# Pooling layer of a three-layer transformer: the trailing mean as one product of 144 columns per token block, on top of a zero product

## The chip, the cores and the metric

The kernel runs on one core of a Trainium2 chip. The metric is the device time of one execution in microseconds; the shown time is the median of three runs. One further execution was profiled, and all rows below are from it.

## The reference, cut to what matters

Three layers run one after the other on 512 tokens of 1024 channels. The change touches the mixer of the third one, the pooling layer: per group of 256 channels a trailing mean over 2, 4, 8 or 16 tokens, minus the token itself, then a 256x256 map and a scale per channel.

```python
def mixer_pool(h, w_groups, scale):
    c = jnp.cumsum(hf, axis=1)
    count = jnp.arange(1, S + 1, dtype=jnp.float32)
    for gi, w in enumerate(POOL_WINDOWS):              # 2, 4, 8, 16
        sl = slice(gi * POOL_GROUP, (gi + 1) * POOL_GROUP)
        cg = c[..., sl]
        lag = jnp.pad(cg, ((0, 0), (w, 0), (0, 0)))[:, :S]
        mean = (cg - lag) / jnp.minimum(count, float(w))[None, :, None]
        outs.append(mean - hf[..., sl])
    pooled = jnp.stack(outs, axis=2).astype(h.dtype)
    y = jnp.einsum('bsgc,gcd->bsgd', pooled, w_groups).reshape(B, S, D)
    return y * scale
...
    h = h + rmsnorm(m, g[1])
    u = rmsnorm(h, g[2])
    h = h + rmsnorm(swiglu(u, ...), g[3])
```

## The kernel before, in words

The kernel is one long program for five engines, written out by hand: `FLOW` lists the stages, each engine has its own queue of instructions for every stage, and semaphores tie the queues together. Activations lie channels first: 8 tiles (`m`) of 128 channels by 512 tokens. Weights come in 233 units of 128x1024 numbers. SyncE loads a unit into one of four buffers `raw`. ScalarE makes its high part (`split_hi`, L818) and counts `hi_done`. VectorE makes the low part by subtraction (`split_lo`, L1330) and counts `lo_done`, which TensorE waits for and which frees the `raw` buffer for the unit four further on. In one earlier stage GpSimd makes some of the low parts (L757). A weight product of this kind has operands of type float32r (the number type whose products TensorE makes in one pass); operands of plain float32 take two passes, so each such product in the source is two matmul rows in the trace.

The pooling layer (`pool_layer` in the queues of ScalarE, VectorE and TensorE) does the map first and the mean afterwards. `linear(half, g)` maps two token blocks of 128 for a group, with tokens as output rows. `z_out(half, g)` moves the mapped block out of PSUM to `zt`, times the row's reciprocal root mean square: L994 on ScalarE, L1605 on VectorE, shared out by the table `ACT_Z`. Each z_out counts `zc_act` or `zc_dve`. Then, for each of the eight channel tiles `m`, TensorE multiplies `zt` with `band`, a banded matrix of plain float32 that holds the mean and the subtracted token: the main product covers the 128 columns of a block's own tokens (L2535), and the carry product covers the first 16 columns of the next block, which the block's last tokens reach into (L2539). The first product of a tile clears the PSUM bank. This part is called the averaging loop below. Before the first product of tile `m`, TensorE waits for `zc_act` and `zc_dve` up to group `m // 2` of the second half.

Behind each tile, ScalarE squares it (L852), and VectorE adds the square to a sum (L1339) and copies the first four tiles out (L1941). When the sum is complete, TensorE adds it over the channels (L2153), ScalarE takes the root (L1021, L1023), VectorE scales and adds the residual (L1616, L1620), ScalarE prepares the operand of the next stage (L1031), and TensorE starts on that stage (L2139). Between, TensorE runs products whose results nobody reads (`keep_clock`, L2119).

The units of the stage behind the pooling layer are counted from `FIRST["pool"] + 2`. They are called unit +2, +3, +4 and so on here. +2 to +4 are what `keep_clock` and the first products of the next stage read. They are split inside the pooling layer.

Of the kernel before, what the change touches and what calls it, by code (L numbers as in the profile page):

```python
# [27 lines left out]
P = 128  # L28
S = 512
# [9 lines left out]
NB = S // P  # L39
# [4 lines left out]
NPOOL, MAXW = 4, 16  # L44
GW = D // NPOOL
RAW, SPL = 4, 2
# [4 lines left out]
FIRST, COUNT, ORDER = {}, {}, [p[0] for p in PHASES]  # L51
# [70 lines left out]
def build(nc, xT, vecs, conv, sinks, w_alpha2, pe, cmp_w1, cmp_w2, weights, yT, flow=FLOW):  # L122
    f32, f32r = mybir.dt.float32, mybir.dt.float32r
    ALU, ACT, AX = mybir.AluOpType, mybir.ActivationFunctionType, mybir.AxisListType
# [4 lines left out]
    with ctx:  # L129
        def sb(name, shape, dt=f32, where=ctx):  # L130
            return where.enter_context(nc.sbuf_tensor(name, shape, dt))
# [5 lines left out]
        raw = [sb(f"raw{i}", [P, WU * P]) for i in range(RAW)]  # L137
# [11 lines left out]
        convw = sb("convw", [P, 4 * 2 * KF])  # L149
        epsc = sb("epsc", [P, 32])  # L150
        invc = sb("invc", [P, MAXW])

        ffn = ExitStack()
        ahi = sb("ahi", [P, KF * S], f32r, ffn)
# [8 lines left out]
        band = sb("band", [P, 2 * NPOOL, P + MAXW], f32, ffn)  # L163
# [211 lines left out]
        def whigh(n):  # L375
            if n == 2:
                return oh[:, 0:WU * P]
            if n == POOL_1:
                return map_pieces(alo, 8)
            if n in KEPT:  # L380
                return hhi[:, KEPT[n] * WU * P:KEPT[n] * WU * P + WU * P]
            return ahi[:, (16 + 2 * EXTRA[n]) * S:(18 + 2 * EXTRA[n]) * S] if n in EXTRA else whi[n % SPL][:, :]

        def wlow(n):
            if n == 2:
                return ol[:, 0:WU * P]
            if n == POOL_1:
                return map_pieces(alo, 12)
            if n in KEPT:
                return hlo[:, KEPT[n] * WU * P:KEPT[n] * WU * P + WU * P]  # L390
            return alo[:, (16 + 2 * EXTRA[n]) * S:(18 + 2 * EXTRA[n]) * S] if n in EXTRA else wlo[n % SPL][:, :]
# [265 lines left out]
        def _(pool):  # L657
# [5 lines left out]
            def fill(ins):  # L663
                n_filled[0] += 1
                ins.then_inc(filled, 1)

                pool.wait_ge(filled, n_filled[0])
# [4 lines left out]

            fill(pool.memset(ones[:, :], 1.0 / D))
            fill(pool.memset(epsc[:, :], EPS))
            fill(pool.memset(ident[:, :], 0.0))
            select(ident[:, :], [[-1, P]], 0, 1, ALU.not_equal, 1.0).then_inc(const_0, 1)
            for c in range(MAXW):
# [92 lines left out]
            if "pool" in names:  # L770

                pool.wait_ge(unit_done, FIRST["down_b0"] + 1)
                for g in range(NPOOL):
                    w = 2 << g
                    pair = band[:, 2 * g:2 * g + 2, :]
                    fill(pool.memset(pair, 1.0 / w))
                    fill(pool.tensor_copy(band[:, 2 * g + 1, 0:w - 1], invc[:, 0:w - 1]))
                    fill(select(pair, [[0, 2], [-1, P + MAXW]], w - 1, 1, ALU.is_ge, 0.0))
                fill(select(band[:, :, :], [[0, 2 * NPOOL], [1, P + MAXW]], 0, -1, ALU.is_ge, 0.0))
                pool.tensor_tensor(band[:, :, 0:P], band[:, :, 0:P],  # L780
                                   ident[:, :].rearrange("p (a t) -> p a t", a=1).broadcast_to([P, 2 * NPOOL, P]),
                                   ALU.subtract).then_inc(B["band"], 1)
            if "up_b1" in names:
                lower(8)
            if flow[-1] == ("post", LAST):
# [540 lines left out]
        def _(dve):  # L1326
            def split_lo(n, i):

                dve.wait_ge(hi_done, n + 1 + 4 * i)
                dve.tensor_tensor(wlow(n), raw_of(n), whigh(n).bitcast(f32),  # L1330
                                  ALU.subtract).then_inc(lo_done, 1)
# [214 lines left out]
            def handover():  # L1546

                p = "down_b0"

                def half_lower(m, half):  # L1550

                    dve.wait_ge(h_hi, H_BASE[6] + KD * half + m + 1)
                    dve.scalar_tensor_tensor(out=half_tile(alo, m, half), in0=half_tile(x, m, half), scalar=col(GAIN[6], m),
                                             in1=half_tile(ahi, m, half).bitcast(f32), op0=ALU.mult, op1=ALU.subtract
                                             ).then_inc(h_lo, 1)

                def half_post(m, half):

                    y = half_tile(mt, m, half)
                    dve.scalar_tensor_tensor(out=y, in0=y, scalar=col(GAIN[5], m), in1=rstd[:, HALVES[half]],  # L1560
                                             op0=ALU.mult, op1=ALU.mult).then_inc(post_done, 1)
                    if m >= 1:
                        half_lower(m - 1, half)
                    dve.wait_ge(post_done, X_BASE[5] + KD * half + m + 1)
                    dve.tensor_tensor(half_tile(x, m, half), half_tile(x, m, half), y, ALU.add).then_inc(x_done, 1)

                half_summed(p, 6, 0)
                def squares_added_up(i):

                    dve.wait_ge(bsq_ready, 2 * i + 2)  # L1570
                    if i >= 2:
                        dve.wait_ge(squares_sum, i - 1)
                    dve.tensor_tensor(square_pair(0), square_pair(0), square_pair(i), ALU.add).then_inc(squares_sum, 1)

                half_summed(p, 7, 0)
                dve.wait_ge(rstd_ready, 6)
                dve.wait_ge(evac[p], KD)
                for m in range(KD):
                    half_post(m, 0)
                    if m == 1:  # L1580
                        split_lo(POOL_0, 0)
                    if m == 4:
                        squares_added_up(1)
                        half_summed(p, 6, 1)
                    if m == 6:
                        squares_added_up(2)
                half_summed(p, 7, 1)
                half_lower(KD - 1, 0)
                squares_added_up(3)
                split_lo(POOL_1, 0)  # L1590
                dve.wait_ge(rstd_ready, 7)
                dve.wait_ge(evac[p], KD + 2)
                for m in range(KD):
                    half_post(m, 1)
                half_lower(KD - 1, 1)
                dve.wait_ge(rcol_ready, 1)
                z_out(0, 2)
                z_out(0, 3)
                clear_sum("pool")
# [328 lines left out]
            def pool_layer():  # L1928
                p = "pool"
                handover()  # L1930
                split_lo(FIRST[p] + 2, 0)
                dve.tensor_tensor(gscale[:, :], vec[:, VEC["pool_scale"]:VEC["pool_scale"] + KD],
                                  vec[:, VEC[GAIN[7]]:VEC[GAIN[7]] + KD], ALU.mult).then_inc(B["gscale"], 1)
                dve.wait_ge(rcol_ready, 2)
                for g in range(NPOOL):
                    z_out(1, g)
                split_lo(FIRST[p] + 3, 0)
                for m in range(KD):
                    residual(p, m, MEAN_BANK[m])
                    if m < DVE_COPIES:  # L1940
                        dve.tensor_copy(tile(mt, m), ps[:, MEAN_BANK[m], :]).then_inc(B["mcopy"], 1)  # L1941
                    if m == 2:
                        split_lo(FIRST[p] + 4, 0)
                split_lo(FIRST[p] + 5, 0)
                dve.wait_ge(B["gscale"], 1)
                dve.wait_ge(B["mcopy"], DVE_COPIES)
# [19 lines left out]
        def _(pe_):  # L1966
# [503 lines left out]
            def pool_layer():  # L2470
# [55 lines left out]
                for m in range(KD):  # L2526
                    g = m // 2
                    pe_.wait_ge(B["zc_act"], act_z(1, g))
                    pe_.wait_ge(B["zc_dve"], dve_z(1, g))
                    if m >= 6:  # L2530

                        pe_.wait_ge(B["mcopy"], 2 if MEAN_BANK[m] == MEAN_BANK[1] else 1)
                    for b in range(NB):
                        c = b * P
                        last = pe_.matmul(ps[:, MEAN_BANK[m], c:c + P], zt[:, b, m * P:m * P + P],  # L2535
                                          band[:, 2 * g + (b == 0), 0:P], start=b == 0, stop=False)
                    for b in range(1, NB):
                        c = b * P
                        last = pe_.matmul(ps[:, MEAN_BANK[m], c:c + MAXW], zt[:, b - 1, m * P:m * P + P],  # L2539
                                          band[:, 2 * g, P:P + MAXW], start=False, stop=b == NB - 1)  # L2540
                    last.then_inc(B["mean"], 1)

            for kind, what in flow:
# [110 lines left out]
```

## Time and profile before

| | us |
|---|---|
| median of three runs | 1665.63 (1665.28 to 1665.72) |
| the profiled execution's own time | 1666.04 |
| its span in the trace | 1664.3 |
| TensorE busy | 1632.6 (98%) |
| VectorE busy | 883.8 (53%) |
| ScalarE busy | 709.9 (43%) |
| GpSimd busy | 166.3 (10%) |
| averaging loop, first to last product | 1272.2 to 1284.7 of the span |

Busy times of TensorE are of pipelined products with modelled ends, each row reaching into the next. The spacing of the starts is what a product takes. The span leaves out some 1.7 us of the execution's own time.

### The profile page before, as it was taken

The page shows a single profiled execution, that of the slowest core. Times are in us where ns is not written, and L with a number is a line of the kernel's source. Part 1 is how long each engine was busy: PE and PEld are TensorE (multiplying, and loading weights), DVE is VectorE, ACT ScalarE, POOL GpSimd, SP SyncE. Part 2 cuts the span into 40 slices and gives each one's busy share as a digit, 9 for nine tenths or more (in the row PEclk, how much of TensorE's full clock was granted, in tenths as well). Part 3 has the DMA queues.
Part 4 walks back from the last instruction along what each step waited for, and adds up shares of the span by engine and source line. Part 5 has one row for each costly group of instructions (what it writes and reads, how often), then busy time and mean ns, then how long its engine had stood idle before and what let it go on. Part 6 is the DMA issues. An engine that isn't in the chain of part 4 may idle for free.

```text
span 1664.3 us, 22461 instructions
## 1 busy us (share of the span) xinstructions
PE 1632.6 (98%) x8132; PEld 1355.0 (81%) x8132; DVE 883.8 (53%) x1470; ACT 709.9 (43%) x1205; POOL 166.3 (10%) x249
## 2 busy tenths in 40 slices
PE   8999999999999999999899999999999999999997
PEld 7777788888888887888777888888899788888887
DVE  5644667777743356676646544443248644444233
ACT  4555454444432226677646332232236523233231
POOL 2011000000000022445402000002000200000001
PEclk9999999999999999999999999999999999999999
DMA  5211223332333242121112233233331123333331
GB/s 181 89 39 40 88 89 101 101 98 91 92 107 93 89 129 77 39 64 52 52 55 85 89 100 98 91 101 98 92 114 59 56 90 99 101 90 100 101 102 51
DMA packets 57159, 144.89 MB, mean 87 GB/s; under 512 B 14160, under 2 KB 20976, under 8 KB 57088
## 3 DMA queue, kind: packets, MB, share of 16 engines
q1 hardware_dynamic: 55680, 141.58, 27.5%
q0 software_dynamic: 688, 1.26, 0.4%
q8 instruction: 45, 0.74, 0.2%
q10 hardware_dynamic: 720, 1.10, 0.2%
q14 instruction: 26, 0.21, 0.0%
HBM read 138.67 MB, written 2.10 MB: 85 GB/s over the span
## 4 chain that ended last, share of the span: by engine, by line
PE 92%; ACT 3%; DVE 3%; issue 1%; DMA 1%; ACTq 0%; POOL 0%; DVEq 0%
PE ps L1970 26%; PE ps L1972 25%; PE ps L1971 25%; PE ps L2071 1%; PE ps L2070 1%; PE ps L2069 1%; PE ps L2139 1%; PE ps L2363 1%; PE ps L2378 1%; PE ps L2416 1%; PE ps L2364 1%; PE ps L2129 1%; DMA x<-xT 1%; PE ps L2535 0%; PE ps L2202 0%
## 5 line engine op out<-in xcount | busy, mean ns | idle before, releaser
L1970 PE MATMUL ps<-hhi,whi 128*128 128x512 f32 x1400 | 553.1, 395 | 3.0 <-DVE wlo L1330 2.3
L1971 PE MATMUL ps<-hlo,whi 128*128 128x512 f32 x1400 | 546.3, 390 | 0.0
L1972 PE MATMUL ps<-hhi,wlo 128*128 128x512 f32 x1400 | 546.1, 390 | 0.0
L1330 DVE TENSOR_TENSOR wlo<-raw,whi 128x1024 fp32r<-128x1024 f32 x229 | 280.5, 1225 | 451.4 <-ACT whi L818 448.6
L818 ACT ACTIVATE whi<-raw 128x1024 fp32r<-128x1024 f32 x242 | 255.9, 1057 | 518.9 <-PE ps L1972 518.7
L1970 PEld LDWEIGHTS ps<-hhi,whi 128*128 128x128 f32 x1400 | 263.4, 188 | 66.6 <-issue 8.2
L1972 PEld LDWEIGHTS ps<-hhi,wlo 128*128 128x128 f32 x1400 | 263.4, 188 | 55.7
L1971 PEld LDWEIGHTS ps<-hlo,whi 128*128 128x128 f32 x1400 | 263.7, 188 | 53.8 <-issue 1.2
L1970 PE MATMUL ps<-ahi,whi 128*128 128x512 f32 x432 | 168.0, 389 | 0.0
L1971 PE MATMUL ps<-alo,whi 128*128 128x512 f32 x432 | 168.0, 389 | 0.0
L1972 PE MATMUL ps<-ahi,wlo 128*128 128x512 f32 x432 | 168.0, 389 | 0.0
L879 ACT ACTIVATE ahi<-gated 128x512 f32 (+1 forms) x66 | 41.7, 632 | 148.3 <-DVE gated L1446 148.3
L1417 DVE TENSOR_TENSOR pre<-ps,rstd 128x512 f32<-128x512 f32 x132 | 90.1, 684 | 21.9 <-ACT rstd L1023 14.3
L1970 PEld LDWEIGHTS ps<-ahi,whi 128*128 128x128 f32 x432 | 81.1, 188 | 17.0
L1971 PEld LDWEIGHTS ps<-alo,whi 128*128 128x128 f32 x432 | 81.1, 188 | 16.8
L1972 PEld LDWEIGHTS ps<-ahi,wlo 128*128 128x128 f32 x432 | 81.1, 188 | 16.7
L1448 DVE TENSOR_TENSOR alo<-gated,ahi 128x512 f32 (+1 forms) x66 | 45.7, 693 | 59.3 <-ACT ahi L879 59.3
L1236 ACT ACTIVATE pth<-ps 128x128 fp32r<-128x128 f32 (+3 forms) x96 | 36.6, 433 | 39.6 <-PE ps L2378 39.0
L1339 DVE TENSOR_TENSOR sq<-sq 128x512 f32<-128x512 f32 x44 | 30.3, 689 | 35.0 <-ACT sq L852 24.8
L1870 DVE TENSOR_TENSOR ptl<-ps,pth 128x128 fp32r<-128x128 f32 (+3 forms) x96 | 42.9, 486 | 11.0 <-ACT pth L1236 10.8
L868 ACT ACTIVATE cvt<-pre,convw 128x512 f32<-128x512 f32 x44 | 35.4, 807 | 28.8 <-DVE pre L1417 28.8
L1242 ACT ACTIVATE pB<-pB,nmB 128x512 f32<-128x512 f32 (+3 forms) x80 | 44.2, 557 | 6.6 <-DVE nmB L1855 6.5
(358 smaller groups left out, 2022.1 us busy)
## 6 DMA issues: line engine op xcount, KB each, us to landing
raw<-w_up_b SPq DMA_DIRECT2D x88, 512.0 KB, 3.5
raw<-w_up_a SPq DMA_DIRECT2D x44, 512.0 KB, 3.4
raw<-w_in_b SPq DMA_DIRECT2D x23, 512.0 KB, 3.8
raw<-w_in_a SPq DMA_DIRECT2D x19, 512.0 KB, 3.5
raw<-w_down_b SPq DMA_DIRECT2D x16, 512.0 KB, 3.5
raw<-w_out_a SPq DMA_DIRECT2D x8, 512.0 KB, 3.5
raw<-w_down_a SPq DMA_DIRECT2D x8, 512.0 KB, 3.5
raw<-w_out_b SPq DMA_DIRECT2D x8, 512.0 KB, 3.7
```

The lines of the kernel that those rows point to most:

```text
L818: act.activation(whigh(n), raw_of(n), ACT.Copy).then_inc(hi_done, 1)
L868: act.activation(cvt[:, s, :], pre[:, s, :], ACT.Identity, bias=convw[:, bass.ds(3 * 2 * KF + c + fi, 1)], scale=convw[:, bass.ds(2 * 2 * ...
L879: act.activation(tile(ahi, f + fi), gated[:, :], ACT.Copy).then_inc(k["ahi"], 1)
L1236: act.activation(pth[:, j % 2, 0:n, s % 2, :], ps[:, 2 + s % 2, 0:n * P].rearrange("p (j q) -> p j q", q=P), ACT.Copy).then_inc(B["hi"], 1)
L1242: act.activation(ptile(s)[:, 0:w], ptile(s)[:, 0:w], ACT.Exp, scale=-1.0, bias=nmB[:, s:s + 1], accum_out=smB[:, s:s + 1]).then_inc(B["p"], 1)
L1330: dve.tensor_tensor(wlow(n), raw_of(n), whigh(n).bitcast(f32), ALU.subtract).then_inc(lo_done, 1)
L1417: dve.tensor_tensor(pre[:, u % 2, :], ps[:, u % 4, :], rstd[:, :], ALU.mult).then_inc(evac[p], 1)
L1448: dve.tensor_tensor(tile(alo, f + fi), gated[:, :], tile(ahi, f + fi).bitcast(f32), ALU.subtract).then_inc(k["alo"], 1)
L1870: dve.tensor_tensor(ptl[:, j % 2, 0:n, s % 2, :], ps[:, 2 + s % 2, 0:n * P].rearrange("p (j q) -> p j q", q=P), pth[:, j % 2, 0:n, s % 2, ...
L1970: pe_.matmul(out, wh, hi, start=start, stop=False)
L1971: pe_.matmul(out, wh, lo, start=False, stop=False)
L1972: return pe_.matmul(out, wl, hi, start=False, stop=stop)
```

## The change

Each tile of the averaging loop begins with one float32r product of a zero column with a zero row, both repeated by a stride of zero, over all 512 columns of the bank; it clears the bank. The products with `band` add to it: one of 144 columns for each of the first three token blocks and one of 128 for the last. The zeros are set at the start of the program, on GpSimd. Four low parts of units are made at other places: unit +2 on VectorE ahead of the z_outs of the first half and no longer behind them, unit +3 on GpSimd, unit +4 on VectorE behind the last sum and no longer in the middle of the sums, with a wait for `lo_done`; unit +5 stays where it was, behind unit +4.

```diff
+        zero = sb("zero", [P, 32], f32r)
...
             fill(pool.memset(epsc[:, :], EPS))
+            fill(pool.memset(zero[:, :].bitcast(f32), 0.0))
             fill(pool.memset(ident[:, :], 0.0))
...
+                n = FIRST["pool"] + 3
+                pool.wait_ge(hi_done, n + 1)
+                pool.wait_ge(lo_done, n)
+                pool.tensor_tensor(wlow(n), raw[n % RAW][:, :], whigh(n).bitcast(f32), ALU.subtract).then_inc(lo_done, 1)
...
                 half_lower(KD - 1, 1)
+                split_lo(FIRST["pool"] + 2, 0)
                 dve.wait_ge(rcol_ready, 1)
                 z_out(0, 2)
                 z_out(0, 3)
...
                 handover()
-                split_lo(FIRST[p] + 2, 0)
                 dve.tensor_tensor(gscale[:, :], vec[:, VEC["pool_scale"]:VEC["pool_scale"] + KD],
...
                     z_out(1, g)
-                split_lo(FIRST[p] + 3, 0)
                 for m in range(KD):
                     residual(p, m, MEAN_BANK[m])
...
-                    if m == 2:
-                        split_lo(FIRST[p] + 4, 0)
+                dve.wait_ge(lo_done, FIRST[p] + 4)
+                split_lo(FIRST[p] + 4, 0)
                 split_lo(FIRST[p] + 5, 0)
...
+                    pe_.matmul(ps[:, MEAN_BANK[m], :], zero[:, 0:1].broadcast_to([P, P]), zero[:, 0:1].broadcast_to([P, S]),
+                               start=True, stop=False)
                     for b in range(NB):
-                        c = b * P
-                        last = pe_.matmul(ps[:, MEAN_BANK[m], c:c + P], zt[:, b, m * P:m * P + P],
-                                          band[:, 2 * g + (b == 0), 0:P], start=b == 0, stop=False)
-                    for b in range(1, NB):
-                        c = b * P
-                        last = pe_.matmul(ps[:, MEAN_BANK[m], c:c + MAXW], zt[:, b - 1, m * P:m * P + P],
-                                          band[:, 2 * g, P:P + MAXW], start=False, stop=b == NB - 1)
+                        c, w = b * P, P + MAXW if b < NB - 1 else P
+                        last = pe_.matmul(ps[:, MEAN_BANK[m], c:c + w], zt[:, b, m * P:m * P + P],
+                                          band[:, 2 * g + (b == 0), 0:w], start=False, stop=b == NB - 1)
                     last.then_inc(B["mean"], 1)
```

TensorE's queue at the start of the averaging loop, before (`b_zc_dve` and `b_zc_act` count the z_outs; a plain float32 product is one row here and two in the trace):

```order
4004 L2502 MATMUL ps<-alo,ahi 128x256
4005 L2535 MATMUL ps<-band,zt 128x128 [waits b_zc_dve,b_zc_act,b_band]
4006 L2535 MATMUL ps<-band,zt 128x128 x3
4007 L2539 MATMUL ps<-band,zt 128x16 x3
4008 L2535 MATMUL ps<-band,zt 128x128 [waits b_zc_dve,b_zc_act]
```

The same place after the change:

```order
4004 L2507 MATMUL ps<-alo,ahi 128x256
4005 L2538 MATMUL ps<-zero 128x512 [waits b_zc_dve,b_zc_act,b_band]
4006 L2542 MATMUL ps<-band,zt 128x144 x3
4007 L2542 MATMUL ps<-band,zt 128x128
4008 L2538 MATMUL ps<-zero 128x512 [waits b_zc_dve,b_zc_act]
```

Seven products of a tile have become five, and the zero product now carries the waits, so it can't start ahead of them.

VectorE's queue from the last piece of the second half's operand to the first sum, before (TENSOR_TENSOR from `raw` is a split, TENSOR_SCALAR to `zt` a z_out):

```order
897 L1553 SCALAR_TENSOR_TENSOR alo<-x,vec,ahi 128x256 [waits h_hi]
898 L1605 TENSOR_SCALAR zt<-ps,rcol 128x256 [waits b_z,rcol_ready]
...
902 L1495 MEMSET sq 128x512
903 L1330 TENSOR_TENSOR alo<-raw,ahi 128x1024 [waits hi_done,zeroed]
904 L1932 TENSOR_TENSOR gscale<-vec 128x8
905 L1605 TENSOR_SCALAR zt<-ps,rcol 128x256 [waits unit_done,b_z,rcol_ready]
...
909 L1330 TENSOR_TENSOR alo<-raw,ahi 128x1024 [waits hi_done]
910 L1339 TENSOR_TENSOR sq<-sq 128x512 [waits sq_ready]
```

The same place after the change:

```order
897 L1559 SCALAR_TENSOR_TENSOR alo<-x,vec,ahi 128x256 [waits h_hi]
898 L1336 TENSOR_TENSOR alo<-raw,ahi 128x1024 [waits hi_done]
899 L1612 TENSOR_SCALAR zt<-ps,rcol 128x256 [waits b_z,rcol_ready]
...
903 L1501 MEMSET sq 128x512
904 L1938 TENSOR_TENSOR gscale<-vec 128x8 [waits zeroed]
905 L1612 TENSOR_SCALAR zt<-ps,rcol 128x256 [waits unit_done,b_z,rcol_ready]
...
909 L1345 TENSOR_TENSOR sq<-sq 128x512 [waits sq_ready]
```

The split of unit +2 stands now in front of the four z_outs of the first half, and that of unit +3 is gone from this queue.

VectorE's queue from the third tile's copy to the residual, before:

```order
915 L1941 COPY mt<-ps 128x512
916 L1330 TENSOR_TENSOR alo<-raw,ahi 128x1024 [waits hi_done]
917 L1339 TENSOR_TENSOR sq<-sq 128x512 [waits sq_used,sq_ready]
918 L1941 COPY mt<-ps 128x512
919 L1339 TENSOR_TENSOR sq<-sq 128x512 [waits sq_used,sq_ready] x4
920 L1330 TENSOR_TENSOR wlo<-raw,whi 128x1024 [waits hi_done]
921 L1616 SCALAR_TENSOR_TENSOR ps<-mt,gscale,ps 128x512 [waits rstd_ready,b_mcopy,b_gscale]
```

The same place after the change:

```order
914 L1946 COPY mt<-ps 128x512
915 L1345 TENSOR_TENSOR sq<-sq 128x512 [waits sq_used,sq_ready]
916 L1946 COPY mt<-ps 128x512
917 L1345 TENSOR_TENSOR sq<-sq 128x512 [waits sq_used,sq_ready] x4
918 L1336 TENSOR_TENSOR alo<-raw,ahi 128x1024 [waits hi_done,lo_done]
919 L1336 TENSOR_TENSOR wlo<-raw,whi 128x1024 [waits hi_done]
920 L1623 SCALAR_TENSOR_TENSOR ps<-mt,gscale,ps 128x512 [waits rstd_ready,b_mcopy,b_gscale]
```

The split between the third copy and the fourth sum is gone, and two splits in place of one stand between the last sum and the scaling of the residual.

## Rows read from the trace of the kernel before

**Rows 1.** Page, its first line
```profile
span 1664.3 us, 22461 instructions
```

**Rows 2.** Chain that ended last, 1270 to 1292 us: start, us, what
```profile
1272.23 1.11 PE ps L2535 x8
...
1284.90 0.70 ACT sq L852
...
1285.62 0.70 DVE sq L1339
...
1286.37 1.14 PE ps L2153 x2
...
1291.36 0.70 PE ps L2139 x2
```

**Rows 3.** Timeline of TensorE: start, us, engine, line, instruction, forms, idle before
```profile
1271.95 0.28 PE L2502 MATMUL ps<-alo,ahi 128*128 128x256 f32 x1
...
1272.21 1.13 PE L2535 MATMUL ps<-band,zt 128*128 128x128 f32 x8
...
1273.77 1.14 PE L2535 MATMUL ps<-band,zt 128*128 128x128 f32 x8
...
1274.74 0.74 PE L2539 MATMUL ps<-band,zt 128*128 128x16 f32 x6
...
1284.71 1.41 PE L2119 MATMUL ps<-ahi 128*128 128x512 f32 x5
```

**Rows 4.** Windows: us, busy by engine, PEclk, DMA share, GB/s
```profile
1272.00:1285.00 13.00, 13.00 (x115) 12.83 (x115) 12.29 (x20) 8.90 (x16) 0.00 (x0) 1.00 0.40 123
```

**Rows 5.** Duration of plain float32 passes by line, ns min/median/max
```profile
L2539 PE MATMUL ps<-band,zt x48: 182/262/263, 1273.2 to 1284.6; 128*128 128x16 f32 x48
L2535 PE MATMUL ps<-band,zt x64: 275/275/356, 1272.2 to 1284.0; 128*128 128x128 f32 x64
L2153 PE MATMUL ps<-sq,ones x8: 590/592/697, 221.3 to 1286.9; 128*128 128x512 f32 x8
```

**Rows 6.** Timeline of TensorE: float32r products, the first one behind plain float32
```profile
1264.98 0.36 PE L2500 MATMUL ps<-whi,ahi 128*128 128x256 f32 x1
...
1265.18 0.28 PE L2501 MATMUL ps<-whi,alo 128*128 128x256 f32 x1
...
1301.31 0.39 PE L2139 MATMUL ps<-hhi,ahi 128*128 128x512 f32 x1
1301.53 0.39 PE L2139 MATMUL ps<-hhi,alo 128*128 128x512 f32 x1
```

**Rows 7.** Instructions of L2445: float32r product whose weights are a repeated column
```profile
L2445 PE MATMUL ps<-csr,esel x8: 392/398/494, 661.9 to 821.3; 128*128 128x512 f32 x8
```

**Rows 8.** Timeline of VectorE around the averaging loop
```profile
1270.18 1.65 DVE L1605 TENSOR_SCALAR zt<-ps,rcol 128x256 f32<-128x256 f32 x4
...
1272.40 1.23 DVE L1330 TENSOR_TENSOR alo<-raw,ahi 128x1024 fp32r<-128x1024 f32 x1
...
1273.62 1.65 DVE L1605 TENSOR_SCALAR zt<-ps,rcol 128x256 f32<-128x256 f32 x4
...
1286.23 1.22 DVE L1330 TENSOR_TENSOR wlo<-raw,whi 128x1024 fp32r<-128x1024 f32 x1
1288.98 0.75 DVE L1616 SCALAR_TENSOR_TENSOR ps<-mt,gscale,ps 128x512 f32<-128x512 f32 x1 [1.54 <-ACT ps L1023]
```

**Rows 9.** Timeline of ScalarE: z_outs of the second half, one copy behind the squares
```profile
1271.27 1.57 ACT L994 ACTIVATE zt<-ps,rcol 128x256 f32<-128x256 f32 x4
...
1283.92 0.59 ACT L854 ACTIVATE mt<-ps 128x512 f32<-128x512 f32 x1
```

**Rows 10.** Instructions of L757: split on GpSimd in the earlier stage
```profile
L757 POOL TENSOR_TENSOR wlo<-raw,whi x13: 2377/2403/2408, 654.2 to 812.0; 128x1024 fp32r<-128x1024 f32 x13
```

**Rows 11.** Timeline of the start: GpSimd's constants, the first wait of TensorE
```profile
3.65 0.20 POOL L675 MEMSET ident<- 128x128 f32 x1
...
13.16 0.50 PE L1970 MATMUL ps<-hhi,whi 128*128 128x512 f32 x1 [0.23 <-DVE hlo L1528]
```

## The prediction

> **What bounds the kernel now.** [...] Busy times of TensorE overlap, so I went on to the chain that ended last. It runs through all products of the loop, then ScalarE's square of tile 7 at 1284.90, VectorE's sum at 1285.62, the sum over channels at 1286.37 and, by way of root and residual, to the next stage's first product at 1291.36 [rows 2]. The reader should see that between 1284.7 and 1291.4 the path is a chain of single instructions, and that from 1291.36 TensorE is the bound again. So what the last tile gains or loses is handed on whole. It starts for a reason too: the last product of the map was issued at 1271.95, the first of the loop at 1272.21, 0.26 us later, with ScalarE's z_outs just before it [rows 3, 9]. The four z_outs at 1271.27 are (1.57-0.44)/3 = 0.38 us apart, taking 0.44 for one, an estimate; the second, which the first tile needs, ends near 1272.09. VectorE's four z_outs of the first half end at 1270.18+1.65 = 1271.83 [rows 8]: 0.3 us earlier. Both are waited for.
>
> **The products, per tile.** Before: tiles start 1.56 us apart (1272.21 to 1273.77), and from the first to the first product behind the loop it is 1284.71-1272.21 = 12.50 for eight [rows 3], 1.5625 each. Of the second tile, the carry passes begin at 1274.74, so 8 passes of 128 columns take 0.97, 0.121 each, and the 6 passes of 16 columns the rest, 0.59 or 0.098 each [rows 3]. [...] What is added:
> - 16 more columns on six passes. Passes last 275 ns at 128 columns and 592 at 512 [rows 5]: 0.83 ns a column, 0.013 us for 16. Six passes of 144 columns: 6 x 0.134 = 0.81 us. Two of 128: 0.24.
> - The zero product. The trace has no product with two repeated operands. A float32r product of 512 columns takes 1301.53-1301.31 = 0.22 to 0.23 us [rows 6]; one whose weights are a repeated column lasts 398 ns, no longer than the 390 of others [rows 6, 7]. But it will stand behind plain float32. The five float32r products of L2119 behind the loop take 1.41 us with an end of 0.39, so four spacings are 1.02 [rows 3]; three of 0.228 leave 0.336 for the first, 0.108 more than usual. At 1264.98 a product of 256 columns behind plain float32 shows the same: next start 0.20 later, duration 0.36 against 0.28 [rows 6], 0.08 more. Bounds for the zero product: 0.228 (no bubble) to 0.43 (its columns pass at plain float32's 0.83 ns, as they would if repeated reads were slow). I take 0.336, the row nearest to it in position.
>
> Sum per tile: 0.336+0.81+0.24 = 1.386. Saved: 0.176, times eight 1.41 us.
>
> [...]
>
> **The loop's start.** The split of unit +2 moves ahead of VectorE's four z_outs of the first half. A split holds VectorE for 1.14 us (1273.62-1272.40 is 1.22, and some 0.08 of it, an estimate, is the small product for the scale between) [rows 8]. The z_outs then end at 1271.83+1.14 = 1272.97, and behind them stands the first tile, whose `zc_dve` counts them. With 0.05 us for the hand-over (the sum at 1285.62 plus its 0.70 to 1286.37) [rows 2] the zero product starts at 1273.03 and no longer at 1272.21: 0.82 us lost. The z_outs of the second half aren't later: the same work stands before them in another order, and their start stays at 1273.6 [rows 8]. Tile 2, which needs two of them, begins at 1273.03+2 x 1.39 = 1275.8, long after.
>
> **The last tile.** It ends at 1273.03+8 x 1.386 = 1284.12 in issues, against 1284.71: 0.59 earlier. The last pass has 128 columns in place of 16, and lasts 275 ns against 182 at the least [rows 5]; less the 0.02 longer spacing, the square comes some 0.07 later behind it than before. Net gain at ScalarE: 0.5 us, to 1284.4.
>
> **What else moves.** ScalarE has 0.59 for the square and about as much for the copy per tile, 1.2 us [rows 2, 9], under TensorE's 1.39: no new bound. VectorE loses two splits inside the loop, 2.3 us, so its sums follow the squares. Behind the last sum now stand two splits, not one: from 1285.7 to 1285.7+2 x 1.14+0.08 = 1288.1, while the scaling of the residual becomes possible at 1288.98-0.5 = 1288.5. This split is free, with 0.4 us to spare; before, 1.54 us lay idle there [rows 8]. Without that cover it would cost up to 1.14. GpSimd's split takes 2.40 us [rows 10]. It starts behind the split of unit +2, near 1271.4, and ends near 1273.8. GpSimd is idle then [rows 4]; the next work in its queue is the low half of the next stage's operand, made behind the residual; and VectorE waits for it only at 1285.7. SyncE's queue: the load into unit +3's buffer starts some 2.5 us earlier, that into unit +4's, with all queued behind it, some 5 us later; what is queued there already waited for unit +5's split at 1286.23+1.14. The later load is of unit +8, six units of 24 products of 0.228 us after 1291.36, that is some 33 us on: free. The extra constant delays GpSimd's other constants by one memset, at most the 0.20 us of the one at 3.65; TensorE's first wait at 13.16 is for VectorE and 0.23 long, so this is hidden [rows 11].
>
> **The sum.** -1.41+0.82+0.07 is -0.5 us. The span goes from 1664.3 [rows 1] to 1663.8 and the profiled execution's time from 1666.04 to 1665.5. The median of the runs stands 0.41 below that execution, so the forecast is 1665.63-0.5 = 1665.1.
>
> **Rivals.**
> - *No bubble in front of the zero product.* [...] Against it: rows 3 and 6. Then each zero product takes 0.228, eight save 0.86 more: 1664.3. Chance 0.2.
> - *The zero product is slow, and the kernel gets slower.* One mechanism: its moving operand has a stride of zero, which no row shows. At 0.43 us a product the tile takes 1.48, the loop saves 0.66, and the late start outweighs it: +0.2 us, 1665.9. If it ran in two passes as plain float32 does (2 x 0.43), the loop would take 2.8 us more than before, 3.7 with the start: 1669.3. The point from which it decides is 0.336+0.5/8 = 0.40 us each. Chance 0.12 for the first, 0.02 for the second.
> - *The gain is lost behind the loop.* If VectorE's two splits overrun the root by more than the 0.4 us to spare, or ScalarE's splits of units +4 and +5 hold up a square, the gain shrinks towards nothing: 1665.6. For it: four engines follow each other closely here. Against: the sums above. Chance 0.1.
> - *The clock falls.* TensorE stands still some 0.95 us before the first tile, 0.82 more than now. Before, that gap was 0.15, and the loop kept 1.00 [rows 3, 4]. Were the clock at its lower level through the loop, 11 us of passes would take up to 22: 1676. Chance 0.01. [...]
> - The forecast itself: 0.55.
>
> **Numbers.** All likely cases lie between 1664.3 and 1665.9. The three runs differ by 0.44 us, and one program differs from another in its layout in memory and code; I add 1 us on either side, an estimate from the 0.76 us between the lowest run and the profiled one. Range 1663.3 to 1666.8; outside are the two-pass case, the clock and more of such shifts. No measurement of this kernel could tell a change under 0.2% (3.3 us) from none, and only the two-pass case and the clock pass it: slower 0.03. Even a zero product of no cost would save 8 x (1.5625-1.05) = 4.1, less the late start and end of 0.9, 3.2 us: faster 0.02, for what I can't see. Within: 0.95.
>
> **What would show it.** In the trace after: zero products some 0.34 us from start to next start behind plain float32; passes of 144 columns 0.134 apart and 288 ns long; tiles 1.39 apart; the loop's first product at about 1273.0, released by VectorE's z_out, and the square of tile 7 at 1284.4; GpSimd's split of 2.4 us beside the loop; VectorE idle for 0.4 us before the residual. The prediction is wrong if tiles are more than 1.5 us apart, if the first product still starts at 1272.2, or if L1616's counterpart waits for VectorE itself.

## The result, and the profile after

The changed kernel takes 1673.43 us (1672.83 to 1673.49, five runs) against 1665.63 for the kernel before (1664.97 to 1665.84, five runs): 7.8 us slower, a ratio of 1.0047 [1.0034, 1.0059]. Forecast were 1665.1 and a range up to 1666.8. The sign and the size are both wrong.

The profile's page gives the span and the busy times of the products of the three down stages (`ahi` and `alo` are their moving operand, `whi` and `wlo` their weights; busy us, mean ns):

```profile
span 1671.6 us, 22383 instructions
...
L1977 PE MATMUL ps<-ahi,wlo 128*128 128x512 f32 x432 | 170.6, 395 | 0.0
L1975 PE MATMUL ps<-ahi,whi 128*128 128x512 f32 x432 | 170.6, 395 | 0.0
L1976 PE MATMUL ps<-alo,whi 128*128 128x512 f32 x432 | 170.6, 395 | 0.0
```

The averaging loop, on TensorE's timeline:

```profile
1278.63 0.28 PE L2507 MATMUL ps<-alo,ahi 128*128 128x256 f32 x1
1279.79 0.45 PE L2538 MATMUL ps<-zero 128*128 128x512 f32 x1 [0.87 <-DVE zt L1612]
1280.08 1.12 PE L2542 MATMUL ps<-band,zt 128*128 128x144 f32 x8
1280.95 0.46 PE L2538 MATMUL ps<-zero 128*128 128x512 f32 x1
...
1289.17 1.39 PE L2124 MATMUL ps<-ahi 128*128 128x512 f32 x5
1290.92 1.12 PE L2158 MATMUL ps<-sq,ones 128*128 128x512 f32 x2 [0.36 <-DVE sq L1345]
...
1295.92 0.47 PE L2144 MATMUL ps<-hhi,ahi 128*128 128x512 f32 x1 [0.66 <-ACT hhi L1037]
```

That a product of plain float32 is made in two passes and one of float32r in one is read from the counts of rows: in the kernel before the 32 main products are 64 rows and the 24 carry products 48 [rows 5]; here the 32 products with `band` are 64 rows of L2542, eight in 1.12 us, and the eight zero products are 8 rows of L2538.

And VectorE behind the loop:

```profile
1290.18 0.69 DVE L1345 TENSOR_TENSOR sq<-sq 128x512 f32<-128x512 f32 x1 [0.49 <-ACT sq L858]
1290.78 1.22 DVE L1336 TENSOR_TENSOR alo<-raw,ahi 128x1024 fp32r<-128x1024 f32 x1
1291.92 1.22 DVE L1336 TENSOR_TENSOR wlo<-raw,whi 128x1024 fp32r<-128x1024 f32 x1
1293.54 0.76 DVE L1623 SCALAR_TENSOR_TENSOR ps<-mt,gscale,ps 128x512 f32<-128x512 f32 x1 [0.40 <-ACT ps L1029]
```

The first thing to read is an absolute time. The last product of the map starts at 1278.63, where the kernel before had 1271.95 [rows 3]: 6.7 us are gone before the first changed instruction of the pooling layer. From there to the next stage's first product it is 1295.92-1278.63 = 17.29 us, against 1291.36-1271.95 = 19.41 [rows 2, 3]. So the part that the change edits has won 2.1 us, and the kernel has lost some 9.4 us elsewhere, where no instruction was changed: 7.3 in the span = 6.7-2.1+2.7.

The windows of 40 us in a down stage say where. The kernel before, then the changed one (us, busy by engine, PEclk, DMA share, GB/s; the number in brackets counts products):

```profile
1560.00:1600.00 40.00, 40.00 (x178) 33.15 (x177) 11.61 (x11) 10.91 (x14) 0.00 (x0) 1.00 0.30 93
```

```profile
1100.00:1140.00 40.00, 40.00 (x178) 33.07 (x177) 18.97 (x23) 11.87 (x16) 0.00 (x0) 1.00 0.30 92
1560.00:1600.00 40.00, 40.00 (x174) 32.15 (x173) 9.83 (x10) 10.17 (x13) 0.00 (x0) 1.00 0.30 92
```

At the same clock and with no idle time, TensorE gets through 174 products in place of 178 in the down stage, while in the up stage (1100 to 1140) it keeps its 178. The down stages read `ahi` and `alo`; the up stages read `hhi` and `hlo`. What lies between these two pairs in memory is the new tensor. The down stage's group that the page above shows with 395 ns had 389 in the kernel before:

```profile
L1970 PE MATMUL ps<-ahi,whi 128*128 128x512 f32 x432 | 168.0, 389 | 0.0
```

### The profile page after: what moved, and what is told of

It reads as the page before. It is cut to its first block, busy times and chain, and to the rows that moved or that the text cites. A ratio compares the mean times of both kernels' runs of the same rounds, so it can differ in the third digit from the quotient of the medians.

```text
span 1671.6 us, 22383 instructions
## 1 busy us (share of the span) xinstructions
PE 1639.0 (98%) x8092; PEld 1350.9 (81%) x8092; DVE 885.2 (53%) x1469; ACT 710.6 (43%) x1205; POOL 168.6 (10%) x251
## 4 chain that ended last, share of the span: by engine, by line
PE 92%; DVE 3%; ACT 3%; issue 1%; DMA 1%; ACTq 0%; POOL 0%; DVEq 0%
PE ps L1975 26%; PE ps L1976 25%; PE ps L1977 25%; PE ps L2144 1%; PE ps L2074 1%; PE ps L2076 1%; PE ps L2075 1%; PE ps L2383 1%; PE ps L2368 1%; PE ps L2421 1%; PE ps L2369 1%; PE ps L2134 1%; DMA x<-xT 1%; PE ps L2182 0%; PE ps L2207 0%
```

## The experiments

The theory formed from this: the 128 bytes a partition of `zero` push all tensors allocated behind it (`ahi`, `alo`, and what shares their space) 128 bytes on, and a product with one operand in front of it and one behind is then slower. The places follow from the order and sizes of the allocations: in the kernel before, `whi`, `wlo`, `x`, `hhi`, `hlo`, `ahi`, `alo` and `oh` all start at 128 modulo 256 bytes of a partition. The rival: the changed instructions or their code cost the time. Each experiment is compared with the kernel before on its own chip: 1666.05 for experiments 1 to 4, 1665.78 for 5, 9, 10 and 11, 1665.24 for 6, 7, 8 and 12.

**1. Placement without the change.** Only this line is added to the kernel before:

```diff
         invc = sb("invc", [P, MAXW])
+        unused = sb("unused", [P, 32])
```

> The kernel before, with nothing added but an unused tensor of 128 bytes a partition at the place where the change allocates its zeros, so that every tensor behind it (ahi, alo, oh and the rest) stands 128 bytes further on and whi, wlo, hhi, hlo stay. Theory P (placement): the change lost its time because products with one operand in front of the new tensor and one behind it read more slowly, 395 against 389 ns on the 1296 products of the three down stages. Then this kernel has all of the loss and none of the loop's gain: about 9.5 us slower, 1675. Rival C (code): the loss is of the changed instructions, and this kernel takes 1665.6 within 0.5.

Measured: 1675.72 against 1666.05, ratio 1.0057 [1.0040, 1.0074], 9.7 us slower. The down products last 395 ns. A program with the very instructions of the kernel before is slower than the changed one. From the map's last product (1279.12) to the next stage's first (1298.52) it has 19.40 us, as before. So the loss needs no changed instruction.

**2. The change without the placement.** `epsc` used one of its 32 columns:

```diff
-        epsc = sb("epsc", [P, 32])
+        epsc = sb("epsc", [P, 16])
+        zero = sb("zero", [P, 16], f32r)
...
-        zero = sb("zero", [P, 32], f32r)
```

> The changed kernel, with the tensor of zeros in the unused half of the constant epsc, so that no tensor stands elsewhere than in the kernel before. Theory P: the loss goes and the loop's gain of some 2.2 us is left, 1663.4, and the down stages' products last 389 ns again. Rival C: 1673.4 as the changed kernel.

Measured: 1664.19 against 1666.05, ratio 0.9989 [0.9979, 0.9999]: 1.9 us faster. Its page, the answer to the rows above:

```profile
span 1661.8 us, 22383 instructions
...
L1975 PE MATMUL ps<-ahi,whi 128*128 128x512 f32 x432 | 168.0, 389 | 0.0
```

**3 to 5. Which property of the place.** The same unused tensor with 64 columns (256 bytes) in the same place; with 32 columns in front of all other tensors; and one of 32 columns on either side of `whi` and `wlo`, which moves the weights' tensors alone by half a period of 256:

```diff
+        unused = sb("unused", [P, 32])
         whi = [sb(f"whi{i}", [P, WU * P], f32r) for i in range(SPL)]
         wlo = [sb(f"wlo{i}", [P, WU * P], f32r) for i in range(SPL)]
+        unused_2 = sb("unused_2", [P, 32])
```

> The kernel before with an unused tensor of 256 bytes a partition at the same place. If the rule is of the distance between the two operands, counted modulo 256 bytes, nothing changes: 1665.6. If any shift of the later tensors costs, or the rule goes by 512 bytes or more, it is as slow as with 128 bytes, 1675, or somewhere between.

> The kernel before with an unused tensor of 128 bytes a partition in front of all others, so that every tensor shifts alike: all starts change from 128 to 0 modulo 256, and no distance between two changes. If the rule is of the distance between operands: 1665.6. If it is of each tensor's own start (0 modulo 256 is slow): all weight products slow down, 5832 of them by 6 ns, some 35 us: 1700.

> The kernel before, with an unused tensor of 128 bytes a partition in front of whi and wlo and another one behind them: whi starts at 0 modulo 256 bytes, while x, hhi, hlo, ahi, alo and all later ones stay at 128. If the cost lies in the distance modulo 256 between TensorE's two operands, every product of 512 columns with whi or wlo pays it, the 4200 with hhi and hlo as well as the 1296 with ahi and alo, 6 ns each: 33 us, so near 1699. If it is something about ahi and alo alone, or about raw's distance from its readers on ScalarE and VectorE, this is near 1666 or at most the 1675 of the first experiment.

Measured: 1665.91, ratio 0.9999 [0.9990, 1.0009], for 256 bytes; 1665.35, 0.9998 [0.9988, 1.0007], for all tensors alike; 1694.86, 1.0176 [1.0160, 1.0192], for the weights apart, 29.1 us. Neither a shift of 256 nor a common one costs anything; moving the weights against everything else costs on every product that uses them. Expected were 33 us by 6 ns each; 29.1 over 5496 products is 5.3. In its page the products with `hhi` are slower too, which they are in no other of these kernels (in experiment 1 and in the kernel before the same group has a mean of 390):

```profile
L1973 PE MATMUL ps<-hlo,whi 128*128 128x512 f32 x1400 | 553.1, 395 | 0.0
```

**6. and 7. Other distances.** 16 and 48 columns, 64 and 192 bytes, where the first experiment had 128:

> The kernel before with an unused tensor of 64 bytes a partition where the change allocates its zeros: ahi and alo then start at 192 modulo 256 bytes, whi and hhi at 128. If the cost goes by the 128-byte half in which two reads meet (bit 7 of their distance), half of each product's reads meet wrongly: about half the loss of 128 bytes, 4.9 us, 1670.7. If it is all or nothing, 1665.8 or 1675.5.

> The same with 192 bytes: ahi and alo start at 64 modulo 256, 192 behind whi, which is 64 short of a whole 256. A rule of the distance that is even about zero gives what 64 bytes give; by halves 1670.7; a rule that any distance but 0 modulo 256 costs in full gives 1675.5.

Measured: 1668.66 for 64 bytes, ratio 1.0018 [1.0009, 1.0027], 3.4 us; 1673.43 for 192, 1.0046 [1.0031, 1.0062], 8.2 us. So 0, 64, 128, 192 and 256 bytes cost 0, 3.4, 9.7, 8.2 and 0. The expected symmetry and the expected halves are both refuted: 192 is not 64, and neither is half of 128. Part of the difference is of the other sign. Products of 256 columns, which the last two down stages have at their ends, get shorter. One of the three largest such groups, in the kernel before and at 192 bytes:

```profile
L2071 PE MATMUL ps<-ahi,hlo 128*128 128x256 f32 x128 | 36.2, 283 | 0.0
...
L2072 PE MATMUL ps<-ahi,hlo 128*128 128x256 f32 x128 | 35.5, 277 | 0.0
```

At 128 bytes this group has 281, at 64 it has 278. So the times are sums of longer and shorter products, and no rule for the distance can be read from them.

At 64 bytes the groups of a down stage (480 to 520 us) are not even alike, though their operands are all equally far apart:

```profile
L1971 PE MATMUL ps<-ahi,whi 128*128 128x512 f32 x59 | 23.2, 394 | 0.0
L1972 PE MATMUL ps<-alo,whi 128*128 128x512 f32 x59 | 22.9, 388 | 0.0
L1973 PE MATMUL ps<-ahi,wlo 128*128 128x512 f32 x58 | 22.7, 392 | 0.0
```

In the same window at 128 all three have 395, at 192 all three 394, in the kernel before 389. By the rows of single lines (min/median/max ns), here the changed kernel, a product can be slow from either side: with `ahi` as the moving operand, and with `oh` (which shares its space) as the weights of a moving `hhi`:

```profile
L1975 PE MATMUL ps<-ahi,whi x432: 392/394/398, 456.9 to 1625.9; 128*128 128x512 f32 x144
...
L1975 PE MATMUL ps<-hhi,oh x8: 392/394/792, 20.6 to 26.4; 128*128 128x512 f32 x8
```

In the kernel before, the same two:

```profile
L1970 PE MATMUL ps<-ahi,whi x432: 389/389/389, 456.1 to 1618.4; 128*128 128x512 f32 x144
...
L1970 PE MATMUL ps<-hhi,oh x8: 387/389/799, 20.7 to 26.3; 128*128 128x512 f32 x8
```

**8. The changed kernel with the allocation moved to the front.** Every instruction is that of the change:

```diff
+        zero = sb("zero", [P, 32], f32r)
         raw = [sb(f"raw{i}", [P, WU * P]) for i in range(RAW)]
...
-        zero = sb("zero", [P, 32], f32r)
```

> The changed kernel, line for line, with the allocation of its zeros moved in front of all others, so that all tensors behind stand 128 bytes further on alike. If only distances between operands count, it takes 1664.2, as with the zeros in epsc's half; if the place of the new tensor itself or any shift costs, up to 1673.4.

Measured: 1663.44 against 1665.24, ratio 0.9987 [0.9978, 0.9996], 1.8 us faster. One line's place makes the difference between 7.8 us slower and 1.8 us faster.

**9. The splits alone.** The kernel before with its old products, and the splits of units +2, +3 and +4 where the change has them (cut: two of the places, read against the kernel before):

```diff
                 half_lower(KD - 1, 1)
+                split_lo(FIRST["pool"] + 2, 0)
                 dve.wait_ge(rcol_ready, 1)
...
-                    if m == 2:
-                        split_lo(FIRST[p] + 4, 0)
+                dve.wait_ge(lo_done, FIRST[p] + 4)
+                split_lo(FIRST[p] + 4, 0)
```

> The kernel before with its old products and the four splits at the changed places. By the prediction's term for the loop's start TensorE begins 0.8 us later and nothing is won: 1666.7 against 1666.0 for the kernel before. Rival: the late start is not on the path: 1666.0.

Measured: 1666.88 against 1665.78, ratio 1.0005 [0.9996, 1.0014]: its own interval can't tell it from nothing. The trace can: the first product starts at 1273.21, 1.16 behind the map's last, and from that last to the next stage 1292.36-1272.05 = 20.31 us go by, 0.90 more than before. On TensorE's timeline:

```profile
1273.21 1.13 PE L2538 MATMUL ps<-band,zt 128*128 128x128 f32 x8 [0.88 <-DVE zt L1610]
```

**10. The products alone.** The new products, zeros in `epsc`'s half, all splits in their old places (cut: two of the places, read against the changed kernel):

```diff
                     z_out(1, g)
+                split_lo(FIRST[p] + 3, 0)
                 for m in range(KD):
...
+                    if m == 2:
+                        split_lo(FIRST[p] + 4, 0)
-                dve.wait_ge(lo_done, FIRST[p] + 4)
-                split_lo(FIRST[p] + 4, 0)
```

> The new products (zeros in epsc's unused half, nothing else placed elsewhere), with the four splits where they were before. TensorE can start the loop 0.8 us earlier than with all of the change, at some 0.26 us behind the map's last product, and its eight tiles take 9.4 us in place of 12.5. Theory D: VectorE now ends last, since its z_outs, two splits, sums and copies are 11.1 us without a gap from their start, which puts the last sum 1.6 us earlier than before: 1664.3. Rival: TensorE still ends last, and the gain is 3 us: 1663.0.

Measured: 1665.91 against 1665.78, ratio 1.0002 [0.9993, 1.0011]. Nothing is won, by neither theory. The stretch from the map's last product to the next stage has 1291.17-1271.61 = 19.56 us. VectorE is late, as theory D has it: ScalarE's square at 1281.50 waited 1.16 us for one of its sums, and the last sum at 1284.48 then waited 0.29 for ScalarE's last square. So the last sum starts only 0.8 us earlier than before (12.87 behind the map's last product, not 13.67) where 1.6 were expected, and then something new happens. TensorE's timeline, then the windows:

```profile
1283.45 1.43 PE L2121 MATMUL ps<-ahi 128*128 128x512 f32 x5 [1.87 <-DVE sq L1341]
...
1285.23 2.07 PE L2155 MATMUL ps<-sq,ones 128*128 128x512 f32 x2 [0.34 <-DVE sq L1341]
1286.31 4.83 PE L2121 MATMUL ps<-ahi 128*128 128x512 f32 x14
```

```profile
1271.00:1284.00 13.00, 11.13 (x82) 10.51 (x81) 12.70 (x22) 9.58 (x17) 0.00 (x0) 1.00 0.39 121
1284.00:1286.00 2.00, 1.66 (x5) 0.87 (x4) 1.71 (x3) 0.94 (x2) 0.00 (x0) 0.76 0.06 12
1286.00:1288.00 2.00, 2.00 (x5) 1.05 (x4) 0.31 (x1) 0.66 (x1) 0.00 (x0) 0.50 0.27 41
```

With fast products and a late VectorE, TensorE stands still for 1.87 us until the sums allow `keep_clock` to start. Behind that the granted clock falls to 0.50 in the window from 1286 to 1288, and the sum over channels, which the residual waits for, lasts 2.07 us where it had 1.12 in the changed kernel. The 0.95 lost there takes back the 0.8 and 0.15 more, which is 19.56 against 19.41. One execution of eleven has a trace; whether the clock falls in the others isn't shown. So the splits' move, which costs 0.9 us by itself, is what lets the products have their gain: with both it is 2.1, with the products alone nothing. Experiment 12 shows which move: not that of unit +2.

**11. The zero product's price.** The kernel of experiment 2 with each zero product issued twice:

```diff
                     pe_.matmul(ps[:, MEAN_BANK[m], :], zero[:, 0:1].broadcast_to([P, P]), zero[:, 0:1].broadcast_to([P, S]),
                                start=True, stop=False)
+                    pe_.matmul(ps[:, MEAN_BANK[m], :], zero[:, 0:1].broadcast_to([P, P]), zero[:, 0:1].broadcast_to([P, S]),
+                               start=False, stop=False)
```

> The changed kernel with its zeros in epsc's unused half and the zero product of each tile issued twice, so that tiles take longer by one zero product that does not stand behind plain float32. [...] If so the second zero product adds 0.213 to 0.23 a tile, 1.8 us in all, and the time is 1666.0 where the kernel without the second one has 1664.2. Rival: a product with both operands repeated is cheap beyond its columns or dear: under 0.1 or over 0.3 a tile.

Measured: 1665.08 against 1665.78, ratio 0.9997 [0.9988, 1.0006]. Each against the kernel before on its own chip, that is 1.2 us more than experiment 2, where 1.8 were expected; times of two chips can't decide over 0.6 us. In the trace the loop takes 1284.22-1273.08 = 11.14 us, where experiment 2 has 1282.05-1272.66 = 9.39: 0.219 for each of the eight. The chain behind shows the same, 19.02 us from the map to the next stage against 17.28. No run shows the 0.213 at the lower end of the expected step; in its place stands this 0.219. A further product of two repeated operands costs no more here than other products of 512 columns, which are 40.00/178 = 0.225 us apart in the up stage's window (1100 to 1140).

**12. The z_outs first.** The kernel of experiment 2 with unit +2's split back behind the z_outs of the first half:

```diff
                 half_lower(KD - 1, 1)
-                split_lo(FIRST["pool"] + 2, 0)
                 dve.wait_ge(rcol_ready, 1)
...
                 handover()
+                split_lo(FIRST[p] + 2, 0)
```

> The changed kernel with its zeros in epsc's unused half, and unit +2's split back behind VectorE's z_outs of the first half; the splits of units +3 and +4 stay where the change put them. The late start of 0.9 us should go: the loop's first product follows the map's last one by 0.26 us, tiles take 1.17, the last sum ends 0.8 us earlier, and the time is 1663.4 against 1664.2 with the split in front. Rival: TensorE gets ahead of VectorE, stands still before keep_clock's products and the granted clock falls as in the run with the loop alone (0.50 there from 1286 to 1288), which takes the gain back: 1664.5 or more.

Measured: 1663.06 against 1665.24, ratio 0.9985 [0.9976, 0.9994], 2.2 us faster, the fastest version here, though its interval overlaps that of 8. The late start is gone (the first product at 1272.07, the map's last at 1271.81), and the clock keeps 1.00. But the stretch to the next stage is 1288.96-1271.81 = 17.15 us, only 0.13 less than in experiment 2 with the split in front (17.28), where the late start alone is 0.9. TensorE's timeline at the end of the loop, then ScalarE's:

```profile
1280.35 0.46 PE L2538 MATMUL ps<-zero 128*128 128x512 f32 x1
...
1282.19 1.43 PE L2124 MATMUL ps<-ahi 128*128 128x512 f32 x5 [0.42 <-DVE sq L1345]
```

```profile
1280.23 0.69 ACT L858 ACTIVATE sq<-ps,vec 128x512 f32<-128x512 f32 x1
1280.82 0.59 ACT L860 ACTIVATE mt<-ps 128x512 f32<-128x512 f32 x1
1281.43 0.69 ACT L858 ACTIVATE sq<-ps,vec 128x512 f32<-128x512 f32 x1
1282.02 0.59 ACT L860 ACTIVATE mt<-ps 128x512 f32<-128x512 f32 x1
1282.50 0.69 ACT L858 ACTIVATE sq<-ps,vec 128x512 f32<-128x512 f32 x1
```

TensorE issues its eighth tile at 1280.35, 8.28 us behind the first, 1.18 a tile, so the tile is issued by 1281.52. In the changed kernel the square follows 0.28 later, which would be 1281.80 here; it comes at 1282.50, without a gap behind ScalarE's copy. ScalarE needs 1.20 us a tile (1280.23 to 1281.43) and now ends last.

That it is late has a reason further up. GpSimd's split, VectorE's first sum and ScalarE's third square in the same kernel:

```profile
1273.62 2.37 POOL L788 TENSOR_TENSOR alo<-raw,ahi 128x1024 fp32r<-128x1024 f32 x1 [125.28 <-DVE alo L1336]
...
1275.05 1.49 DVE L1345 TENSOR_TENSOR sq<-sq 128x512 f32<-128x512 f32 x1
...
1276.63 0.69 ACT L858 ACTIVATE sq<-ps,vec 128x512 f32<-128x512 f32 x1 [0.83 <-DVE sq L1345]
```

The sum began while GpSimd's split ran and took 1.49 us, where the next one takes 0.68; it ended at 1276.54, 0.55 behind the split's end at 1275.99. ScalarE's third square waited 0.83 for it. With GpSimd's split moved behind unit +2's, VectorE thus lost 0.8 us that it doesn't lose in the changed kernel, where the split ran beside the z_outs, four of which took 1.65 us as ever. Without it ScalarE's last square could have come up to 0.7 us earlier, an estimate from 1282.50 less 1281.80. Whether the late start is hidden behind ScalarE's pace or behind this sum is open: no run has the order of experiment 12 and the split of unit +3 elsewhere.

## Why the prediction was wrong, step by step

**The failed step** is the sentence on what else moves: "The extra constant delays GpSimd's other constants by one memset". That is all the text charges for the new tensor. Its place in memory is in no term of the sum; it is only touched under the numbers, as "its layout in memory and code", with an allowance of 1 us. Experiment 1 shows that the place alone costs 9.7 us, experiments 2 and 8 that without it the change wins 1.9 and 1.8, and 3 to 5 that what counts is the distance between the tensors that hold a product's two operands. The affected products add up: 1296 of the down stages by 6 ns (395 against 389) are 7.8 us; those of the layers around, with `oh` or with weights kept in `ahi` and `alo`, make up most of the rest, an inference from the two lines shown under 6 and 7. No row of the trace before could have shown this price, since all these tensors start alike there. But the allocation was in the diff, and ahead of tensors that 1296 of the products read.

**The products' term** had the right sign and was too small. A tile takes 1.174 us (9.39/8), not 1.386, and the gain of the loop is 12.50-9.39 = 3.1 us, not 1.4. All three of its prices were too high, mainly for one reason: the times of starts shift where the width changes. Single passes in the kernel before (one of 128 columns, seven more, the first of 16, five more), then six of 144 in the changed kernel:

```profile
1275.33 0.36 PE L2535 MATMUL ps<-band,zt 128*128 128x128 f32 x1
1275.52 0.94 PE L2535 MATMUL ps<-band,zt 128*128 128x128 f32 x7
...
1276.30 0.18 PE L2539 MATMUL ps<-band,zt 128*128 128x16 f32 x1
1276.33 0.71 PE L2539 MATMUL ps<-band,zt 128*128 128x16 f32 x5
...
1284.77 0.90 PE L2542 MATMUL ps<-band,zt 128*128 128x144 f32 x6
```

With the last pass's duration taken off, the seven are (0.94-0.275)/6 = 0.111 us apart and the five (0.71-0.263)/4 = 0.112. Only the first step of each row differs, 0.19 and 0.03, and the two together are again two passes. So a pass of 16 columns cost as much as one of 128, and 12.50 us are 8 x 14 passes of 0.112; the prediction's 0.121 and 0.098 put the shift into the prices. No run shows what sets the even spacing. The six of 144 are (0.90-0.286)/5 = 0.123 apart, not 0.134. Six of them and two of 128 are some 0.96 of a tile and leave 0.22 for the zero product, which is what experiment 11 measures for one more, not 0.336. By starts alone the zero product has 1281.25-1280.95 = 0.30, but the last pass before it then has 0.03 (its start is 1280.08+1.12-0.275 = 1280.92); the 0.336 was read from behind passes of 16 columns with the same shift in it. The rival without a bubble had this part right, at 0.2, and not the price of the passes. The fourteen even passes could be read from the trace before.

**The loop's start** was right: 1.16 us behind the map's last product in place of 0.26, released by VectorE's z_out with 0.87 idle. Predicted were 0.82 more, measured 0.90, in the changed kernel and by itself in experiment 9.

**The last tile** came out right in size: the square starts 0.28 behind the loop's end, at 1289.45, where it was 0.19; 0.07 more was the forecast. That ScalarE would be no new bound was wrong: at 1.17 us a tile it is level with TensorE now. The square starts where the copy before it ends, 1288.86+0.59, so the agreement with a term for the longer last pass is in part luck. The chain that ended last goes through three of ScalarE's instructions in a row:

```profile
1288.28 0.42 ACT sq L858
1288.86 0.59 ACT mt L860
1289.45 0.70 ACT sq L858
1290.18 0.70 DVE sq L1345
```

**The two splits behind the last sum** were free with 0.40 us to spare, as forecast. GpSimd's split took 2.36 us and nobody waited for its result, but the text had nothing for VectorE beside it: in the changed kernel the small product for the scale took 0.38 us in place of 0.16, which costs nothing there, and in experiment 12 a sum lost 0.8. **The clock** did not fall in the changed kernel: it was 1.00 in every window of 2 us from 1278 to 1292, with 0.87 us of standstill before the loop. It fell in experiment 10, behind a standstill of 1.87 us, to 0.76 and then 0.50 in windows of 2 us, as the rival has it (its 22 us for 11 fit this 0.50, though no run had it in the loop), but at the loop's end, which the prediction had not considered.

Together the edited part was forecast at -0.5 us and has -2.1. What was not in the sum at all has +9.4.

## What to carry to other kernels

A new tensor is an edit to every tensor allocated behind it. Allocate small additions in front of all large ones (128 bytes there had a ratio of 0.9998) or in steps of 256 bytes (0.9999; 128 in the middle had 1.0057; behind all of them moves nothing either, but wasn't tried), and look at absolute times in the trace first: a shift before the first changed instruction can't come from the instructions. A small lengthening of all products of a stage, here 389 to 395 ns, with no wait, is its sign, and padding the kernel before by the same bytes is a test of one line.

Price products from whole runs of equal ones, or from both sides of a change of width: a single step between starts can hold a shift, here 0.08 us either way.

And when TensorE's part of a stage shrinks, ask at the same time whether the engines behind it let it go on: products and splits were worth nothing and less than nothing apart (for the products, with the clock's fall in it), and 2.1 us together.

## What the runs showed of the hardware that was not expected

- The speed of a float32r product of 512 columns depends on how far apart its two operands lie in a partition, as far as tried repeating after 256 bytes: one shift by 256, and two common ones by 128, changed nothing. In the windows of a down stage the means are 389 ns at 0 and 256, 395 at 128, 394 at 192, and 394, 388 and 392 by line at 64. Products of 256 columns go the other way, 283 ns at 0, 278 at 64, 281 at 128 and 277 at 192 in one group. The whole kernel pays 0, 3.4, 9.7, 8.2 and 0 us for 0, 64, 128, 192 and 256. Why these differ stays open: it was not tried.
- Repeating one element for both operands by a stride of zero made a product of 512 columns no slower: 0.219 us, where products without it are 0.225 us apart (178 in the 40 us from 1100 to 1140).
- In the averaging loop a pass of plain float32 with 16 columns takes as long as one with 128, 0.112 us; one of 144 columns takes 0.123.
- An instruction of VectorE that combines two tensors of SBUF, begun while GpSimd's split runs, ended only 0.5 us behind that split: the sum of experiment 12 with 1.49 us in place of 0.68, and in the kernel before one product of 64x512 (L1781, `fks`) in three of its eight places, 1.75 us in place of 0.69. The z_outs, which read PSUM, kept their 1.65 for four.
